# Self-attention under the weight stream: the softmax division of a half of the scores is placed ahead of the next pair's rotation on VectorE

## The reference

```python
def dilated_branch(q, k, v, window, dilation):
    ...
    s = jnp.einsum('bhrnqd,bhrnkd->bhrnqk', qb, kw) * (HEAD_DIM ** -0.5)
    s = jnp.where(jnp.asarray(valid), s, -jnp.inf)
    m = jnp.max(s, axis=-1)
    p = jnp.exp(s - m[..., None])
    den = jnp.sum(p, axis=-1)
    num = jnp.einsum('bhrnqk,bhrnkd->bhrnqd', p, vw)
...
def dilated_attention(q, k, v, positions):
    qf = rotary_2(q.astype(jnp.float32), positions)
    kf = rotary_2(k.astype(jnp.float32), positions)
    ...
    o = num_acc / den_acc[..., None]

def second_block(...):
        h = rms_norm(x, mix_norm_g[l])
        u = h @ w_in[l]
        c = conformer_conv(conv_in, ...)
        a = dilated_attention(qkv[0], qkv[1], qkv[2], positions)
        mixed = jnp.concatenate([rms_norm(c, conv_out_g[l]), rms_norm(a, attn_out_g[l])], axis=-1)
        x = x + mixed @ w_out[l]
```

## Time and profile before

| | us |
|---|---|
| median of 3 runs | 3297.31 |
| lowest and highest run | 3296.79, 3300.74 |
| profiled execution, its own time | 3296.27 |
| profiled execution, its span | 3294.5 |
| PE busy in the span | 3012.7 (91%) |
| DVE, ACT, POOL busy | 1241.7 (38%), 1032.2 (31%), 1052.8 (32%) |
| mean granted clock of TensorE | 0.957 of full speed |

### The profile page before, as it was taken

One profiled execution on the slowest core, in us unless ns is written; L12 is line 12 of the kernel. 1 busy time (PEld: TensorE's weight loads), 2 busy tenths in 40 slices (PEclk: granted clock), 3 DMA queues, 4 the chain that ended last, 5 costly groups with the idle time before them and its releaser, 6 DMA issues. The chain is left out here.

```text
span 3294.5 us, 48855 instructions
## 1 busy us (share of the span) xinstructions
PE 3012.7 (91%) x20726; PEld 2278.3 (69%) x20727; DVE 1241.7 (38%) x1769; ACT 1032.2 (31%) x1516; POOL 1052.8 (32%) x637
## 2 busy tenths in 40 slices
PE   6997999989999699799998999989889988999996
PEld 4776978878888577687887888857667764444542
DVE  2248424334430224842334443047664213222222
ACT  3443233333332244323333333253354321111111
POOL 2353224434444234322443444423234211001000
PEclk8998999989999899899999999989999988999998
DMA  3220022212222212002221222221112126999994
GB/s 128 77 71 18 4 81 96 85 68 99 102 95 85 102 64 71 30 4 82 96 84 65 102 92 102 88 86 53 52 64 90 64 83 266 386 400 402 399 380 174
DMA packets 52912, 402.72 MB, mean 122 GB/s; under 512 B 7008, under 2 KB 8160, under 8 KB 12512
## 3 DMA queue, kind: packets, MB, share of 16 engines
q1 hardware_dynamic: 52704, 399.72, 31.6%
HBM read 397.60 MB, written 2.10 MB: 121 GB/s over the span
## 5 line engine op out<-in xcount | busy, mean ns | idle before, releaser
L1138 POOL TENSOR_TENSOR back_w_lo<-w,back_w_hi 128x1024 fp32r<-128x1024 f32 (+1 forms) x248 | 537.1, 2175 | 752.5 <-ACT back_w_hi L1347 752.4
L1347 ACT CAST back_w_hi<-w 128x1024 fp32r<-128x1024 f32 (+1 forms) x248 | 236.8, 956 | 811.2 <-PE bank L1166 773.8
L1161 PE MATMUL bank<-h_hi,back_w_hi 128*128 128x512 f32 x1056 | 265.8, 394 | 10.7 <-ACT back_w_hi L1347 10.7
L1163 PE MATMUL bank<-h_lo,back_w_hi 128*128 128x512 f32 x1056 | 260.9, 389 | 0.0
L1166 PE MATMUL bank<-h_hi,back_w_lo 128*128 128x512 f32 x1056 | 260.8, 389 | 0.0
L322 POOL TENSOR_TENSOR front_w_lo<-w,front_w_hi 128x1024 fp32r<-128x1024 f32 x68 | 167.0, 2458 | 247.3 <-ACT front_w_hi L499 247.3
L1161 PEld LDWEIGHTS bank<-h_hi,back_w_hi 128*128 128x128 f32 x1056 | 200.0, 190 | 56.0 <-ACT back_w_hi L1347 12.8
L2977 PE MATMUL bank<-moe_w,moe_hg 128*64 128x512 f32 x1024 | 232.5, 597 | 0.8 <-issue 0.8
L1828 POOL TENSOR_TENSOR mid_w_lo<-w,mid_w_hi 128x1024 fp32r<-128x1024 f32 x62 | 150.2, 2425 | 245.6 <-ACT mid_w_hi L2197 245.2
L1163 PEld LDWEIGHTS bank<-h_lo,back_w_hi 128*128 128x128 f32 x1056 | 198.3, 188 | 41.3
L1166 PEld LDWEIGHTS bank<-h_hi,back_w_lo 128*128 128x128 f32 x1056 | 198.2, 188 | 41.2
(11 more groups left out here) (520 smaller groups left out, 5718.9 us busy)
## 6 DMA issues: line engine op xcount, KB each, us to landing
moe_w<-in_moe_w SPq DMA_DIRECT2D x128, 1024.0 KB, 11.5
moe_w<-in_moe_w SPq DMA_DIRECT2D x32, 2048.0 KB, 12.0
w<-in_ffn_up SPq DMA_DIRECT2D x44, 1024.0 KB, 4.7
w<-in_w_merge SPq DMA_DIRECT2D x24, 1536.0 KB, 6.3
w<-in_w_in SPq DMA_DIRECT2D x34, 1024.0 KB, 4.7
w<-in_w_mid SPq DMA_DIRECT2D x31, 1024.0 KB, 4.8
w<-in_ffn_down SPq DMA_DIRECT2D x16, 1408.0 KB, 5.8
w<-in_w_out SPq DMA_DIRECT2D x16, 512.0 KB, 4.0
```

Source lines behind the costliest of these rows:

```text
L1138: nc.gpsimd.tensor_tensor(split(B.w_lo, n), raw(n), split(B.w_hi, n).bitcast(F32), ALU.subtract).then_inc(f["w_lo"], 1)
L1161: nc.tensor.matmul(bank, B.w_hi[:, n % 2, k, :], x_hi[:, cols], start=start and k == 0, stop=False)
L1163: nc.tensor.matmul(bank, B.w_hi[:, n % 2, k, :], x_lo[:, cols], start=False, stop=False)
L1347: nc.scalar.copy(split(B.w_hi, n), raw(n)).then_inc(f["w_hi"], 1)
```

## The change

In VectorE's list of a round, `normalise` moves from behind the rotation and the masks to the front of the attention's part, right behind `take_mem_k`. No instruction is added or taken away, and the other engines' lists are the same.

```diff
@@ -2660,15 +2660,15 @@
                     dve.wait_ge(f["done"], n + 1)
                     nc.vector.tensor_tensor(xT[:, n - CROSS_OUT, :], xT[:, n - CROSS_OUT, :], T.ps[n % 2][:, :],
                                             ALU.add).then_inc(f["took"][n % 2], 1)
+                g, step = att_step(n)
+                if step in (1, 2):
+                    normalise(g, step - 1)
                 if n - 1 in TURNED:
                     half_turn(n - 1)
-                g, step = att_step(n)
                 if step in (0, 1):
                     mask_scores(g, step)
                 if n - 1 in TURNED:
                     finish_turn(n - 1)
-                if step in (1, 2):
-                    normalise(g, step - 1)
                 if step in (2, 3):
                     take_swung(g, step - 2)
```

## The result

| | before | changed |
|---|---|---|
| median of six runs, us | 3297.05 | 3279.44 |
| lowest and highest, us | 3294.42, 3300.74 | 3276.18, 3281.23 |
| profiled execution, its span, us | 3294.5 | 3274.4 |

The ratio is 0.9943, with a 95% interval of 0.9931 to 0.9956. The kernel became 17.6 us faster, and the predicted 3280.5 us is 1.1 us off. The two profiled executions differ by 20.1 us; both kernels' runs are spread over 5 to 6 us, so a difference of spans is told here by its parts, which repeat to a few hundredths between the two traces of the changed kernel. Those two traces are themselves 5.2 us apart in their spans (3274.4 and 3279.6 us), and all of it lies ahead of the pairs: the first scores of pair 0 start at 2254.62 us in one and at 2259.85 in the other.

A forecast was written before the change was run, and what follows sets the result against it. TensorE, busy for 91% of the span, was taken as the bound, with six waits for VectorE's division. A gain of 27.4 us less a loss of 10.6 gave 16.8 us less, 3280.5 us, range 3270 to 3287.

The forecast's parts named there:

- The step that carried most: Pairs 0 to 3: asking what ends each division, earlier divisions were to remove 19.7 us of TensorE's idle time.
- the prediction's case: Pair 3: two L2493 start in GpSimd's gap of 0.48 us, so TensorE's wait falls from 8.32 to 2.6 us.
- The late case: Pair 3: GpSimd's subtraction goes first, the second L2493 waits for 2402.8, and 5.2 us of waiting stay.
- The loss: Pairs 4 and 5: half 0's division, held by two subtractions, delays masks; 8.6 us idle plus 2.0 slow clock, 10.6 us.
- the term for the slow clock: Pairs 4 and 5: waits of 7.3 us bring a slow stretch of 2.5 instead of 1.7 and 1.3, 2.0 us more.
- Cover: Pairs 0 to 3: half 0's division, 1.9 us, fits VectorE's idle time ahead of L2461; 0 to 0.4 us of delay.
- rival C: Every pair: half 0's division delays the masks by some 6 us, making the kernel slower at 3313 us; chance 0.03.
- A: Pairs 4 and 5: VectorE does its four scalings in one go, GpSimd waits, nothing is lost; 3269.9 us, chance 0.10.
- B: Pairs 0, 2 and 3: copies L2500 become TensorE's next wait and give back part of the gain; 3287 us, chance 0.10.
- D: Whole kernel: the wait was not VectorE's queue, or gains are lost before the end; 3291 to 3300 us, chance 0.07.

The follow-up runs named there:

- half 0 alone: Against the changed kernel, only the division of step 1 stays ahead of the masks, that of step 2 goes back behind the rotation; ratio 1.0001 to the kernel before.
- half 1 alone: Against the changed kernel, only the division of step 2 stays ahead of the rotation, that of step 1 goes behind the masks; ratio 0.9987 to the kernel before.
- the filled ones: Against the changed kernel, seven matmuls nobody reads were put into TensorE's waits of pairs 4 and 5 ahead of the transposes; ratio 0.9920 to the kernel before.

## Why the prediction was right

**The rows behind the waits.** The step that carried most, to ask for each of the six waits what ends the division, held. Pairs 0, 1 and 2 have 0, 0.47 and 0 us of waiting left (predicted 0.2, 0.4 and 0.2), pair 3 2.24 (2.6). The gains of the four pairs with their clock are 27.7 us against 27.4. That pair 1 gains only through half 0, and pairs 0 and 2 not through it alone, is shown by half 0 alone; that they do not gain through half 1 alone either was not seen ahead.

**Pair 3.** The prediction had L1836 hold the first L2493 to its end and the second slip in 0.06 us before GpSimd's L1828. In the trace the first one starts at 2378.95, as soon as the exponentials are through and 0.2 us before L1836's end, and the transposes start 1.03 us behind it as in pair 0 of the kernel before, so it was not held by an amount that can be seen. L1828 comes at 2379.72, 0.4 us after the second was due:

```profile
2377.88 1.27 POOL L1836 TENSOR_TENSOR mid_qk<-mid_qk,mid_table 128x512 f32<-128x512 f32 x1 [2.21 <-PE bank L1971]
...
2378.74 0.18 DVE L2489 RECIPROCAL mid_st<-mid_st 128x4 f32<-128x4 f32 x1 [0.42 <-ACT mid_sc L2254]
2378.95 3.80 DVE L2493 TENSOR_SCALAR mid_sc<-mid_sc,mid_st 128x512 f32<-128x512 f32 x4
2379.72 2.35 POOL L1828 TENSOR_TENSOR mid_w_lo<-w,mid_w_hi 128x1024 fp32r<-128x1024 f32 x1 [0.56 <-ACT mid_w_hi L2197]
```

The hold falls on the third of the four (2379.76, 2.60 us, in a narrow window), which head 0's transposes do not need. So the prediction's case came, by 0.4 us and not by a hair. The late case with 5.2 us of waiting did not occur in this kernel's two traces.

**Pairs 4 and 5: the mechanism right, its size 2.8 us too large.** The loss was put at 10.6 us and was 7.8. Of that, 1.1 us are idle time: waits grew by 3.71 and 3.75 us and not by 4.3, since four divisions beside two subtractions take 5.90 us and not 4.7 + 1.7 = 6.4; the first one began 0.1 us ahead of GpSimd's first and was not held. The rest, 1.7 us, is the term for the slow clock: 2.0 us more were expected for the longer waits, since the wait of 5.57 us in pair 0 had cost 2.6. It was 0.4: the first transposes and the eight matmuls behind them took 3.10 + 1.76 us before and 3.65 + 1.32 in the changed kernel (pair 4). This term of the prediction let the price of a wait grow with its length, and the windows show what was wrong with that. The first two rows are of the kernel before (pair 0 and pair 4), the third of the changed kernel (pair 4); the figure behind POOL is the granted clock:

```profile
2276.70:2281.80 5.10, 5.09 (x20) 4.78 (x21) 2.75 (x6) 1.17 (x2) 0.00 (x0) 0.50 0.00 0
2439.00:2442.20 3.20, 3.20 (x17) 3.20 (x16) 1.45 (x3) 3.17 (x5) 0.21 (x1) 0.50 0.01 3
```

```profile
2411.50:2414.70 3.20, 0.00 (x0) 0.02 (x1) 1.20 (x4) 3.18 (x7) 0.00 (x0) 0.50 0.00 0
```

In pair 4 of the kernel before the clock was still 1.00 in the wait (2435.3 to 2438.3) and 0.50 for 3.2 us of work behind it. In the changed kernel it was 0.50 already in the last 3.2 us of the wait, where it costs nothing, and for another 3.6 us of work (2414.7 to 2418.3), then 1.00 again. In pair 0 of the kernel before 5.1 us of work lay at 0.50, and half of that is the 2.6 us. So what a wait cost was half of the slow time that fell on work behind it, and in these two kernels that was about the same behind 3.0 and behind 6.7 us.

**Cover.** The division of half 0 in pairs 0 to 3 cost nothing, as said. In pairs 2 and 3 GpSimd held the third and the fourth of the four, as the prediction allowed, 4.83 and 4.89 us for the four, and still inside VectorE's idle time:

```profile
2331.20 4.83 DVE L2493 TENSOR_SCALAR mid_sc<-mid_sc,mid_st 128x512 f32<-128x512 f32 x4
...
2336.08 0.69 DVE L2461 TENSOR_TENSOR mid_rot_tmp<-bank,mid_table 128x512 f32<-128x512 f32 x1
```

L2461 comes right behind, 0.11 us after the scores L1985 have started, as in the kernel before, so it is just not late; 0.4 us more (VectorE's idle time ahead of the first mask) and the masks would have moved. This was nearer to rival C than the prediction's 0 to 0.4 us of delay say: with the 0.2 us of the reciprocal the division filled the 5.00 us of cover in pair 2 whole.

**The rivals.** A (pairs 4 and 5 lose nothing) is out: the masks were late by 5.4 us (6.54 us behind the scores L1985 instead of 1.18). B (a wait for the copies L2500) did not come: the second transposes start with no wait, and the wait of pair 5's scores for L2500 was there before (0.98 us, now 0.92). C and D did not come.

**The sum.** The distances give 19.9 us, the predicted 16.8 lie 3.1 us below, and the medians 17.6 us. The agreement of the medians to 1.1 us is better than the terms deserve; the runs' spread hides the over-sized loss. So the 1.1 us are in part luck. (In the prediction 2.5 - 1.2 for pair 3's clock was added up as 1.2 and not 1.3, which changes nothing.)

## What to carry to other kernels

A wait of the bound engine is worth asking what ends it in each of its instances and not once: the same five instructions moved by the same edit gained 5 to 8 us in four places and lost 4 in two. What an SBUF-to-SBUF instruction of VectorE costs depends on what GpSimd does in that moment, so before one is put ahead of something that TensorE waits for, look at GpSimd's row there; the masks, which read PSUM, took their 0.69 us beside a subtraction and can stand in such places. And two moves on one queue may only pay together, when the first makes the time in which the second escapes a collision.

## What the runs showed of the hardware

In these traces VectorE's divisions and GpSimd's subtractions took turns instruction by instruction when both engines had more to do: 2.57 and 2.61 us for the second and third division beside two subtractions in a row, 0.49 and 0.48 for the first and last. Four divisions took 1.68 us alone, 3.77 beside one subtraction, and 5.90 beside two, while the two subtractions grew from 4.71 to 5.13 us. The Trainium skill (SBUF — State Buffer, Who interferes with whom) says that whoever starts first has the shared pair for the whole instruction and the other is blocked. The traces agree with that for one instruction: a division due in a subtraction ended 0.3 us behind it. They also show that the blocked one was next, ahead of the holder's own following instruction. The reciprocal L2489 was not held: it took 0.17 us at 2401.72 while GpSimd's L1841 ran.

What the slow clock costs behind a wait was not read off the wait's length. In pairs 4 and 5 it is 4.64 to 4.65 us from the start of the first transposes to the start of head 1's where the clock stayed at 1.00 (behind waits of 1.68 and 1.40 us, and behind the filled ones), 6.20 to 6.31 behind six waits of 3.0 us in three traces, 6.29 to 6.92 behind six of 6.75 us in three others, and 6.08 and 6.99 behind 4.61 and 4.74 us. The sixteen transposes alone took 2.37 to 3.09 us behind 2.24 us of waiting (six traces), 2.51 to 3.51 behind 3.0 us, and 3.37 to 3.65 behind 4.3 to 8.3 us; behind a filled wait 1.94. What puts the start of the slow stretch where it lies is not shown here.
